# Stick-breaking weights as products of sigmoids, and two projections by blocks, in a two-block fp32 network

## Chip, cores and metric

The kernel runs on one core of one Trainium2 chip. The metric is the device time in microseconds of one execution, the median of several. PE is TensorE, DVE is VectorE, ACT is ScalarE, POOL is GpSimd, SP is the queue that issues the DMAs.

## What is computed

256 tokens of width 1024 pass through two transformer-like blocks, all in fp32. The first block multiplies a normalised input with a projection of some 15,000 columns and feeds three branches: an mLSTM with four heads of 256, a short convolution, and stick-breaking attention with 16 heads of 64. The change touches the first and the last of these:

```python
# stick-breaking attention, per head; mask[t, s] = s < t
z = einsum('bhqd,bshd->bhqs', qblk, kf)            # q scaled by d ** -0.5
log_beta = log_sigmoid(z)
log_1m = where(mask, log_beta - z, 0.0)
cum = cumsum(log_1m, axis=-1)
log_a = log_beta + cum[..., -1:] - cum
a = where(mask, exp(log_a), 0.0)                   # = sigmoid(z_ts) * prod_{s<j<t} (1 - sigmoid(z_tj))
out = einsum('bhqs,bshd->bqhd', a, vf)

# mLSTM
y_ml = head_rmsnorm(sigmoid(ml_o) * h_tilde, ml_norm_g, ML_HEADS)
```

Gated projections of the branches, an MLP with squared ReLU, and a second block (recurrent, gated-linear and block-sparse attention branches and a gated MLP) follow and are not touched.

## The kernel before

**Groups and units.** `plan_groups` cuts all products with weights into groups of 512 output columns; a group is worked off in units of up to four blocks of 128 rows of the contraction. A weight tile of a unit (128x2048) is loaded by SP into one of three landing buffers, copied by ACT to a rounded leading part `whi` (L1132), and DVE subtracts to get the rest `wlo` (L1566, `split`); both parts have a ring of three. The activations are split the same way, and PE adds three products: leading by leading, leading by rest, rest by leading. A "tok" group (L594 to L596) has tokens on the output's partitions and moves 512 columns per matmul, 24 matmuls a unit. A "feat" group (L602 to L606) has features there and moves 256 columns, 48 matmuls a unit. A third form, `chunk_product`, is used for the groups `sbk`, `mlq` and `mlk`: for each chunk of 128 features, four matmuls of 512 columns multiply `whi` with both parts of the activations side by side (L561), and four of 256 columns `wlo` with the leading part (L566); DVE then adds the two halves with a reduce for each chunk (`take_chunk`, L1625) before it scales the group (L2038).

**Order.** Every engine walks through the units `u = 0, 1, 2, ...`; what else it does is written out between them by the number of the unit. PE runs the product of unit u and then the extra work of u; `between(u, k)` puts work inside a product, before its k-th block. ACT and DVE start an iteration with a few steps, then prepare the weights of unit u+2, then do the rest of the iteration. The split of unit u+2 can begin once PE has finished unit u-1. The units 0 to 11 are `sbq`, `sbk`, `sbv`; `SB0` is 12. Units 12 to 19 are `mlq0`, `mlq1`, `mlk0`, `mlk1`, 20 to 27 `mlv0`, `mlv1`, `mlo0`, `mlo1` (token form), 28 to 31 `scc0`, `scc1` (feature form); `ML0`, where the mLSTM heads begin, is 30.

**Stick-breaking, two heads at a time, with i = u - SB0.** PSUM has four spare banks `M[0..3]`; head h lives in `M[h % 4]`.
- PE, even i: `sb_scores(i)` (L780, L783): the scores with keys on partitions, 384 columns a head, in three 128x128 blocks (the fourth is above the diagonal).
- ACT, odd i: `sb_logs` (L1208 to L1211): Abs, Exp, then Ln, each over 384 elements, with a table load between.
- DVE: `sb_softplus` (L1637); POOL: `keep` (L2278) zeroes the masked half of the two diagonal blocks by an affine select over 256 elements.
- ACT, next even i: `sb_leading` rounds to `sbw_hi` (L1217), DVE: `sb_rest` subtracts (L1642), and PE, at the end of that unit: `sb_remain` (L793, L794) adds the cumulated sums onto the scores by matmuls with a triangle of minus ones and a block of minus ones, for both parts.
- ACT, odd i: `sb_weights` (L1223) takes Exp; POOL masks again; PE, at the end of the odd unit: `sb_values` (L802, L805). Then ACT and DVE take the result in two parts (`sb_result`, L1227, L1647).

PE's order at the end of an even unit is so remainder (heads i-2, i-1), scores (heads i, i+1), and at the end of an odd one values.

**mLSTM output gate.** ACT computes Exp of the negated, scaled `mlo` (L1442); in the units 28 to 31 DVE adds one and takes the reciprocal over 512 elements (`output_gate`, L1677, L1678).

Of the kernel before, what the change touches and what calls it, by code (L numbers as in the profile page):

```python
# [5 lines left out]
F32 = mybir.dt.float32  # L6
# [151 lines left out]
def chunked(name):  # L158

    return name[:3] in ("sbk", "mlq", "mlk")  # L160
# [31 lines left out]
GATE0 = SB0 + SB_H  # L192
# [6 lines left out]
def build(nc, dram, out):  # L199
# [25 lines left out]
    minus_rstd = sb("minus_rstd", [P, TT], side="right")  # L225
# [38 lines left out]
    sbw_hi = sb("sbw_hi", [P, 2, 3 * P], F32R, stack=area)  # L264
    sbw_lo = sb("sbw_lo", [P, 2, 3 * P], F32R, stack=area)
    sums_r = sb("sums_r", [P, 2 * P], F32R, stack=area)
# [17 lines left out]
    sbw = sb("sbw", [P, 2, 3 * P], stack=mix)  # L284
# [66 lines left out]
    def banks(name):  # L351
# [22 lines left out]
    half_in, ones_in, heat_set, minus_ready = (sem(n) for n in ("half_in", "ones_in", "heat_set", "minus_ready"))  # L374
# [7 lines left out]
    sums_ready, sb_hi, sb_lo = sem("sums_ready"), sem("sb_hi"), sem("sb_lo")  # L382
    sb_z, sb_log, sb_t, sb_tm, sb_r, sb_a, sb_am, sb_av, sb_y = (
        sem(n) for n in ("sb_z", "sb_log", "sb_t", "sb_tm", "sb_r", "sb_a", "sb_am", "sb_av", "sb_y"))
# [109 lines left out]
    def _(pe):  # L494
# [271 lines left out]
        def sb_scores(h):  # L766
# [11 lines left out]
            for i in range(2):  # L778
                hs = slice(SB_D * i, SB_D * (i + 1))
                mm(M[(h + i) % 4][:, 0:T], sbkT[hs, c, 0:P], sbqT[hs, c, :], start=True, stop=True)  # L780
            for i in range(2):
                hs = slice(SB_D * i, SB_D * (i + 1))
                mm(M[(h + i) % 4][:, T:T + P], sbkT[hs, c, P:T], sbqT[hs, c, P:T], start=False, stop=True,  # L783
                   skip_group_check=True).then_inc(sb_z, 1)
# [12 lines left out]
        def sb_values(h):  # L797

            pe.wait_ge(sb_am, h + 2)
            to = M[h % 4]  # L800
            for i in range(2):
                mm(to[SB_D * i:SB_D * (i + 1), 0:T], sbv[:, 0, (h + i) * SB_D:(h + i + 1) * SB_D],  # L802
                   sba[:, i, 0:T], start=True, stop=False, skip_group_check=True)
            for i in range(2):
                last = mm(to[SB_D * i:SB_D * (i + 1), P:T], sbv[:, 1, (h + i) * SB_D:(h + i + 1) * SB_D],  # L805
                          sba[:, i, T:3 * P], start=False, stop=True, skip_group_check=True)
# [19 lines left out]
        def ml_scores(h):  # L826
            s, b = M[2 * (h % 2)], M[2 * (h % 2) + 1]
            if h < 2:
                pe.wait_ge(sb_a, SB_H)
# [158 lines left out]
        def between(u, k):  # L988


            if (u, k) == (LAST_U["psc1"], 2):
# [65 lines left out]
        for u in range(NU):  # L1057
# [54 lines left out]
    def _(act):  # L1112
# [89 lines left out]
        def sb_logs(h):  # L1202

            for i in (h, h + 1):
                act.wait_ge(sb_z, i + 1)
                if i >= 2:
                    act.wait_ge(sb_lo, i - 1)
                link(activate(sbw[:, i % 2], M[i % 4][:, 0:3 * P], ACT.Abs))  # L1208
                link(activate(sbw[:, i % 2], sbw[:, i % 2], ACT.Exp, scale=-1.0))
            for i in (h, h + 1):  # L1210
                activate(sbw[:, i % 2], sbw[:, i % 2], ACT.Ln, bias=1.0).then_inc(sb_log, 1)  # L1211

        def sb_leading(h):
            act.wait_ge(sb_tm, h + 1)
            if h >= 2:
                act.wait_ge(sb_r, h - 1)
            activate(sbw_hi[:, h % 2], sbw[:, h % 2], ACT.Copy).then_inc(sb_hi, 1)  # L1217

# [1181 lines left out]
```

## Time and profile before

| | |
|---|---|
| median of 3 runs | 915.6 us (915.51 to 915.62) |
| the profiled execution | 915.87 us, its span 914.2 us |
| PE busy | 903.5 us, 99% of the span |
| DVE / ACT / POOL busy | 605.8 / 489.0 / 44.3 us |
| HBM read | 162 MB, 181 GB/s over the span |
| remainder, scores and values of the 16 heads | between 87 and 208 us of the span |

The span is what the profiler sees of the program; the execution's time holds a little more on either side. Matmuls are pipelined: the duration in a row is the time from a matmul's start to its modelled end, and several are under way at once.

### The profile page before, as it was taken

How to read it: one execution, taken by the hardware profiler on the slowest of the kernel's cores; microseconds unless marked ns; L12 is line 12 of the kernel's file. 1: busy time of each engine (PE TensorE's matmuls, PEld its weight loads, DVE VectorE, ACT ScalarE, POOL GpSimd, SP SyncE). 2: the span in 40 equal slices, each digit the busy share in tenths (PEclk: the TensorE clock that was granted, in tenths of full speed). 3: DMA queues.
4: the chain of work that ended last, by engine and by line, in shares of the span. 5: the costliest groups of instructions: out<-in, count | busy, mean ns of one | idle time of the engine just before them, and what ended most of it. 6: DMA issues, size and time to landing. Idle time of an engine off the chain costs nothing. (4 is left out here: it accounts for less than half of the span.)

```text
span 914.2 us, 12499 instructions
## 1 busy us (share of the span) xinstructions
PE 903.5 (99%) x5137; PEld 779.1 (85%) x5137; DVE 605.8 (66%) x637; ACT 489.0 (53%) x570; POOL 44.3 (5%) x79
## 2 busy tenths in 40 slices
PE   8999999999999999999999999999999999999997
PEld 7988887789998888888888888889987888888886
DVE  5776766567887445556677755557796677777643
ACT  6434787873435433345555543537777765555441
POOL 1110111110010000000000000001000010000000
PEclk9999999999999999999999999999999999999999
DMA  9676453444255565555565556544842475556641
GB/s 301 221 247 214 138 177 125 160 138 139 92 184 184 186 203 201 194 190 201 167 199 187 185 194 203 201 141 144 277 139 92 132 237 185 184 185 207 207 162 47
DMA packets 99438, 163.92 MB, mean 179 GB/s; under 512 B 4856, under 2 KB 37384, under 8 KB 99253
## 3 DMA queue, kind: packets, MB, share of 16 engines
q1 hardware_dynamic: 99380, 163.11, 54.5%
q8 instruction: 41, 0.67, 0.3%
q14 instruction: 17, 0.13, 0.0%
HBM read 162.04 MB, written 3.16 MB: 181 GB/s over the span
## 5 line engine op out<-in xcount | busy, mean ns | idle before, releaser
L1566 DVE TENSOR_TENSOR wlo<-land,whi 128x2048 fp32r<-128x2048 f32 (+2 forms) x152 | 334.9, 2206 | 164.2 <-ACT whi L1132 163.8
L1132 ACT ACTIVATE whi<-land 128x2048 fp32r<-128x2048 f32 (+1 forms) x152 | 280.3, 1847 | 202.1 <-PE acc L596 145.6
L602 PE MATMUL acc<-xT,whi 128*128 128x256 f32 x336 | 97.2, 289 | 0.0
L606 PE MATMUL acc<-xT,wlo 128*128 128x256 f32 x336 | 95.1, 283 | 0.0
L604 PE MATMUL acc<-xT,whi 128*128 128x256 f32 x336 | 95.0, 283 | 0.0
L594 PE MATMUL acc<-whi,xT 128*128 128x512 f32 (+2 forms) x240 | 91.6, 382 | 0.0
L595 PE MATMUL acc<-wlo,xT 128*128 128x512 f32 (+2 forms) x240 | 90.3, 376 | 0.0
L596 PE MATMUL acc<-whi,xT 128*128 128x512 f32 (+2 forms) x240 | 90.1, 376 | 0.0
L637 PE MATMUL acc<-xT,whi 128*128 128x512 f32 x288 | 69.4, 391 | 0.2 <-DVE gu L2234 0.2
L637 PE MATMUL m<-xT,whi 128*128 128x512 f32 x288 | 68.7, 391 | 0.0
L602 PEld LDWEIGHTS acc<-xT,whi 128*128 128x128 f32 x336 | 64.3, 191 | 2.9 <-issue 2.6
L604 PEld LDWEIGHTS acc<-xT,whi 128*128 128x128 f32 x336 | 64.4, 192 | 0.2
L606 PEld LDWEIGHTS acc<-xT,wlo 128*128 128x128 f32 x336 | 64.4, 192 | 0.0
L637 PEld LDWEIGHTS acc<-xT,whi 128*128 128x128 f32 x288 | 52.8, 188 | 10.5 <-DVE gu L2234 0.4
L637 PEld LDWEIGHTS m<-xT,whi 128*128 128x128 f32 x288 | 52.9, 188 | 10.2
L594 PEld LDWEIGHTS acc<-whi,xT 128*128 128x128 f32 x240 | 45.1, 188 | 9.6 <-issue 1.0
L561 PE MATMUL acc<-xT,whi 128*128 128x512 f32 x192 | 53.0, 397 | 0.0
L596 PEld LDWEIGHTS acc<-whi,xT 128*128 128x128 f32 x240 | 45.1, 188 | 8.2
L595 PEld LDWEIGHTS acc<-wlo,xT 128*128 128x128 f32 x240 | 45.1, 188 | 7.7
L594 PE MATMUL acc<-whi,aT_hi 128*128 128x512 f32 x128 | 49.9, 390 | 0.0
L595 PE MATMUL acc<-wlo,aT_hi 128*128 128x512 f32 x128 | 49.8, 389 | 0.0
L596 PE MATMUL acc<-whi,aT_lo 128*128 128x512 f32 x128 | 49.8, 389 | 0.0
(410 smaller groups left out, 1515.0 us busy)
## 6 DMA issues: line engine op xcount, KB each, us to landing
land<-in_w_in SPq DMA_DIRECT2D x55, 1024.0 KB, 5.2
land<-in_w_up SPq DMA_DIRECT2D x16, 1024.0 KB, 5.2
land<-in_w_down SPq DMA_DIRECT2D x16, 1024.0 KB, 5.1
land<-in_w_ffn_gate SPq DMA_DIRECT2D x22, 512.0 KB, 4.1
land<-in_w_ffn_up SPq DMA_DIRECT2D x22, 512.0 KB, 5.3
land<-in_w_ffn_down SPq DMA_DIRECT2D x10, 1024.0 KB, 5.0
land<-in_w_in SPq DMA_DIRECT2D x14, 512.0 KB, 4.7
land<-in_w_out SPq DMA_DIRECT2D x6, 1024.0 KB, 5.0
```

Of the source, the lines that this page charges most:

```text
L561: mm(to, whi[:, s, k, cs], xT[:, k0 + k].rearrange("p a t -> p (a t)"), start=k0 + k == 0, stop=False, skip_group_check=True)
L594: mm(to, xh[:, k0 + k, ts], whi[:, s, k, 0:w], start=first, stop=False)
L595: mm(to, xh[:, k0 + k, ts], wlo[:, s, k, 0:w], start=False, stop=False)
L596: last = mm(to, xl[:, k0 + k, ts], whi[:, s, k, 0:w], start=False, stop=end)
L602: mm(to, whi[:, s, k, cs], xh[:, k0 + k, :], start=first and c % 2 == 0, stop=False, skip_group_check=True)
L604: mm(to, whi[:, s, k, cs], xl[:, k0 + k, :], start=False, stop=False, skip_group_check=True)
L606: last = mm(to, wlo[:, s, k, cs], xh[:, k0 + k, :], start=False, stop=end, skip_group_check=True)
L637: mm(to[:, c, :], whi[:, s, k, c * P:(c + 1) * P], xT[:, k0 + k].rearrange("p a t -> p (a t)"), start=k0 + k == 0, stop=False, skip_group_ ...
L1132: activate(whi[:, u % PARTS, 0:m, 0:w], land[:, u % LANDS, 0:m, 0:w], ACT.Copy).then_inc(hi_ready, 1)
L1566: v.tensor_tensor(wlo[:, u % PARTS, 0:m, 0:w], land[:, u % LANDS, 0:m, 0:w], whi[:, u % PARTS, 0:m, 0:w].bitcast(F32), ALU.subtract).then_ ...
```

## The change

- The scores are computed with queries on the partitions (operands of `sb_scores` swapped), the same number of matmuls and columns.
- `sb_logs`, `sb_leading`, `sb_weights`, `sb_softplus`, `sb_rest`, `sb_remain` and the buffers `sbw_hi`, `sbw_lo`, `sums_r` go.
- ACT: `sb_sigmoids` writes `sigmoid(-z)` to `sbw` and `sigmoid(z)` to `sba`, 384 elements each, two heads, at the start of an odd iteration.
- POOL: `keep` sets the masked part of `sbw` to 1 and that of `sba` to 0, two selects a head.
- DVE: `sb_products`: a scan from the last key to the first multiplies the factors (`renew` restarts the product at the border between the two query blocks), then a product with `sba`. It stands at the start of an odd iteration, ahead of the weight split.
- PE: `sb_turn`, six transposes (three a head) after the first block of the next even unit's product; ACT copies the results out of PSUM (`sb_copy`); `sb_values` stands at the end of that even unit, directly ahead of the scores of the next pair. So a pair is through one unit sooner.
- `mlq` and `mlk` become plain feature-form groups; DVE scales them from PSUM, without the reduces.
- The output gate is ACT's Sigmoid, and DVE's addition and reciprocal go.

```diff
 def chunked(name):
-    return name[:3] in ("sbk", "mlq", "mlk")
+    return name[:3] == "sbk"
...
@@ tensor
-        def sb_remain(h):
-
-            if h == 0:
-                pe.wait_ge(sums_ready, 1)
-            pe.wait_ge(sb_lo, h + 1)
-            z = M[h % 4]
-            for w in (sbw_hi[:, h % 2], sbw_lo[:, h % 2]):
-                mm(z[:, 0:3 * P], sums_r[:, 0:P], w, start=False, stop=True, skip_group_check=True)
-                last = mm(z[:, P:T], sums_r[:, P:], w[:, T:3 * P], start=False, stop=True, skip_group_check=True)
-            last.then_inc(sb_r, 1)
+        def sb_turn(h):
+
+            pe.wait_ge(sb_a, h + 1)
+            for i in range(3):
+                last = nc.tensor.transpose(M[h % 4][:, i * P:(i + 1) * P], sba[:, h % 2, i * P:(i + 1) * P], ident)
+            last.then_inc(sb_at, 1)
...
         def between(u, k):
+            if k == 1 and u - SB0 in range(2, SB_H + 1, 2):
+                sb_turn(u - SB0 - 2)
+                sb_turn(u - SB0 - 1)
...
-            if i % 2 == 0 and 0 <= i <= SB_H:
-                if i >= 2:
-                    sb_remain(i - 2)
-                    sb_remain(i - 1)
-                if i < SB_H:
-                    sb_scores(i)
-            if i % 2 == 1 and 3 <= i <= SB_H + 1:
-                sb_values(i - 3)
+            if i % 2 == 0 and 2 <= i <= SB_H:
+                sb_values(i - 2)
+            if i % 2 == 0 and 0 <= i < SB_H:
+                sb_scores(i)
@@ scalar
+        def sb_sigmoids(h):
 
             for i in (h, h + 1):
                 act.wait_ge(sb_z, i + 1)
                 if i >= 2:
-                    act.wait_ge(sb_lo, i - 1)
-                link(activate(sbw[:, i % 2], M[i % 4][:, 0:3 * P], ACT.Abs))
-                link(activate(sbw[:, i % 2], sbw[:, i % 2], ACT.Exp, scale=-1.0))
+                    act.wait_ge(sb_a, i - 1)
+                    act.wait_ge(sb_at, i - 1)
+                activate(sbw[:, i % 2], M[i % 4][:, 0:3 * P], ACT.Sigmoid, scale=-1.0)
+                activate(sba[:, i % 2], M[i % 4][:, 0:3 * P], ACT.Sigmoid).then_inc(sb_sig, 1)
+
+        def sb_copy(h):
             for i in (h, h + 1):
+                act.wait_ge(sb_at, i + 1)
+                if i >= 2:
+                    act.wait_ge(sb_av, i // 2)
+                activate(sbaT[:, i % 2], M[i % 4][:, 0:3 * P], ACT.Copy).then_inc(sb_ac, 1)
@@ vector
+        def sb_products(h):
+
+            if h == 0:
+                dve.wait_ge(sb_set, 2)
+            dve.wait_ge(sb_kept, 2 * h + 1)
+            link(v.tensor_tensor_scan(sbp[:, h % 2, ::-1], sbw1[:, h % 2, 3 * P:0:-1], renew[:, ::-1], 1.0, ALU.mult,
+                                      ALU.max))
+            dve.wait_ge(sb_kept, 2 * h + 2)
+            v.tensor_tensor(sba[:, h % 2], sba[:, h % 2], sbp[:, h % 2], ALU.mult).then_inc(sb_a, 1)
...
+            if u - SB0 in range(1, SB_H, 2):
+                sb_products(u - SB0 - 1)
+                sb_products(u - SB0)
@@ gpsimd
+        for h in range(SB_H):
+            pool.wait_ge(sb_sig, h + 1)
+            signal(keep(sbw[:, h % 2], ALU.is_gt, -1, 1.0), sb_kept)
+            signal(keep(sba[:, h % 2], ALU.is_gt, -1), sb_kept)
```

How PE's queue moves, at the end of unit 14 and of unit 15. Before:

```order
L566 MATMUL acc<-xT,wlo 128x256 x4
L793 MATMUL m<-sbw_hi,sums_r 128x384
L794 MATMUL m<-sbw_hi,sums_r 128x128
L793 MATMUL m<-sbw_lo,sums_r 128x384
L794 MATMUL m<-sbw_lo,sums_r 128x128
...
L780 MATMUL m<-sbqT,sbkT 128x256 x2
L783 MATMUL m<-sbqT,sbkT 128x128 x2
L561 MATMUL acc<-xT,whi 128x512 x4
...
L802 MATMUL m<-sba,sbv 64x256 x2
L805 MATMUL m<-sba,sbv 64x128 x2
```

The four remainder rows stand twice, once a head. PE's queue now, in unit 14 after its first block of rows, and at the end of the same unit:

```order
L604 MATMUL acc<-xT,wlo 128x256
L788 MATMUL m<-lead,sba 128x128 x6
L600 MATMUL acc<-xT,whi 128x256
L602 MATMUL acc<-xT,whi 128x256
...
L796 MATMUL m<-sbaT,sbv 64x256 x2
L799 MATMUL m<-sbaT,sbv 64x128 x2
L778 MATMUL m<-sbkT,sbqT 128x256 x2
L781 MATMUL m<-sbkT,sbqT 128x128 x2
```

The remainder has left the end of the even unit, the transposes have come into its middle, and the values have moved up from the odd unit to stand ahead of the scores.

DVE's queue for one pair of units (14 and 15) before, with its waits; `land`, `whi`, `wlo` belong to the weights:

```order
L1566 TENSOR_TENSOR wlo<-land,whi 128x2048 [waits landed1,hi_ready]
L1642 TENSOR_TENSOR sbw_lo<-sbw,sbw_hi 128x384 [waits sb_hi] x2
L1566 TENSOR_TENSOR wlo<-land,whi 128x2048 [waits landed2,hi_ready]
L1625 TENSOR_REDUCE mlqT<-acc 128x256 [waits chunk_done] x2
L1637 SCALAR_TENSOR_TENSOR sbw<-m,sbw 128x384 [waits sb_log] x2
L1625 TENSOR_REDUCE mlqT<-acc 128x256 [waits chunk_done]
L1625 TENSOR_REDUCE mlqT<-acc 128x256 [waits units_done]
L2038 SCALAR_TENSOR_TENSOR mlqT<-mlqT,row 128x1024 [waits chunk_read]
```

and now (the scan is the row that writes `sbp`):

```order
L1546 TENSOR_TENSOR wlo<-land,whi 128x2048 [waits landed1,hi_ready]
L1625 TENSOR_TENSOR ysbT_lo<-m,ysbT_hi 128x256 [waits sb_y_hi]
L1618 SCALAR_TENSOR_TENSOR sbp<-sbw,renew 128x384 [waits sb_kept]
L1621 TENSOR_TENSOR sba<-sba,sbp 128x384 [waits sb_kept,dve_step]
L1618 SCALAR_TENSOR_TENSOR sbp<-sbw,renew 128x384 [waits sb_kept]
L1621 TENSOR_TENSOR sba<-sba,sbp 128x384 [waits sb_kept,dve_step]
L1546 TENSOR_TENSOR wlo<-land,whi 128x2048 [waits landed2,hi_ready]
L2014 SCALAR_TENSOR_TENSOR mlqT<-acc,row 128x1024 [waits units_done]
```

The `sbw` work and the reduces are gone; scans and products wait for POOL's `sb_kept` ahead of the weight split of unit 17.

## Rows read from the trace of the kernel before

**Rows 1.** the page: busy time, share and instructions of each engine; the granted clock

```profile
PE 903.5 (99%) x5137; PEld 779.1 (85%) x5137; DVE 605.8 (66%) x637; ACT 489.0 (53%) x570; POOL 44.3 (5%) x79
...
PEclk9999999999999999999999999999999999999999
```

**Rows 2.** waits of PE and its weight loads: us in total, times, longest

```profile
PE m L793 <- DVE sbw_lo L1642: 0.2, 1, 0.2
...
PEld m L793 <- DVE sbw_lo L1642: 1.0, 2, 0.7
```

**Rows 3.** PE timeline after unit 14: start, us, then the instruction

```profile
99.52 0.41 PE L793 MATMUL m<-sbw_hi,sums_r 128*128 128x384 f32 x1
...
100.78 0.70 PE L780 MATMUL m<-sbqT,sbkT 64*128 64x256 f32 x4
...
101.64 1.20 PE L561 MATMUL acc<-xT,whi 128*128 128x512 f32 x4
```

**Rows 4.** PE timeline after unit 22, token form

```profile
157.69 0.33 PE L793 MATMUL m<-sbw_hi,sums_r 128*128 128x384 f32 x1
...
158.87 0.70 PE L780 MATMUL m<-sbqT,sbkT 64*128 64x256 f32 x4
```

**Rows 5.** PE timeline after unit 20: the hole before the remainder

```profile
142.84 0.39 PE L596 MATMUL acc<-whi,xT 128*128 128x512 f32 x1
143.47 0.45 PE L793 MATMUL m<-sbw_hi,sums_r 128*128 128x384 f32 x1 [0.24 <-DVE sbw_lo L1642]
```

**Rows 6.** PE timeline in the second block: six transposes in either stream

```profile
685.99 0.82 PE L876 MATMUL m<-lead,mbs 128*128 128x128 f32 x6
...
686.76 0.28 PE L604 MATMUL acc<-xT,whi 128*128 128x256 f32 x1
...
708.38 0.82 PE L876 MATMUL m<-lead,mbs 128*128 128x128 f32 x6
...
709.27 0.40 PE L595 MATMUL acc<-wlo,y2T_hi 128*128 128x512 f32 x1
```

**Rows 7.** PE timeline after unit 15: a values block

```profile
107.44 0.65 PE L802 MATMUL m<-sba,sbv 128*64 128x256 f32 x4
...
108.24 0.96 PE L561 MATMUL acc<-xT,whi 128*128 128x512 f32 x3
```

**Rows 8.** PE timeline: a chunked unit from its start to the next, and plain matmuls

```profile
36.53 1.09 PE L561 MATMUL acc<-xT,whi 128*128 128x512 f32 x4
...
42.15 1.09 PE L561 MATMUL acc<-xT,whi 128*128 128x512 f32 x4
...
198.83 0.28 PE L602 MATMUL acc<-xT,whi 128*128 128x256 f32 x1
...
200.15 0.28 PE L606 MATMUL acc<-xT,wlo 128*128 128x256 f32 x1
```

**Rows 9.** single lines' instructions: count, ns min/median/max, first and last start

```profile
L1208 ACT ACTIVATE sbw<-m x16: 470/492/500, 89.2 to 189.8; 128x384 f32<-128x384 f32 x16
...
L1211 ACT ACT_TABLE_LOAD  x8: 1283/1283/1283, 91.4 to 190.9; - x8
...
L2278 POOL TENSOR_SCALAR_AFFINE_SELECT sba<-sba x20: 406/408/2083, 103.5 to 241.9; 128x256 f32<-128x256 f32 x20
...
L1642 DVE TENSOR_TENSOR sbw_lo<-sbw,sbw_hi x16: 548/550/553, 98.8 to 199.4; 128x384 fp32r<-128x384 f32 x16
...
L1837 DVE TENSOR_TENSOR_SCAN lw<-lw x2: 664/678/691, 685.9 to 686.5; 128x256 f32<-128x256 f32 x2
```

**Rows 10.** PE timeline in unit 20: 512-column matmuls, eighteen steps

```profile
138.30 0.39 PE L594 MATMUL acc<-whi,xT 128*128 128x512 f32 x1
...
142.39 0.39 PE L594 MATMUL acc<-whi,xT 128*128 128x512 f32 x1
```

**Rows 11.** GpSimd's and VectorE's timelines at 188 us

```profile
188.59 2.56 POOL L2278 TENSOR_SCALAR_AFFINE_SELECT sba<-sba 128x256 f32<-128x256 f32 x2 [6.97 <-ACT sba L1223]
...
188.12 2.29 DVE L1566 TENSOR_TENSOR wlo<-land,whi 128x2048 fp32r<-128x2048 f32 x1 [2.25 <-ACT whi L1132]
```

More of the change, by code:

```diff
@@ L263, in build @@
     early.close()
-    sbw_hi = sb("sbw_hi", [P, 2, 3 * P], F32R, stack=area)
-    sbw_lo = sb("sbw_lo", [P, 2, 3 * P], F32R, stack=area)
-    sums_r = sb("sums_r", [P, 2 * P], F32R, stack=area)
+    sbaT = sb("sbaT", [P, 2, 3 * P], stack=area)
+    sbp = sb("sbp", [P, 2, 3 * P], stack=area)
+    renew = sb("renew", [P, 3 * P], stack=area)
     area.close()
@@ L283, in build @@
     mlo = sb("mlo", [P, TT, D], stack=mix)
-    sbw = sb("sbw", [P, 2, 3 * P], stack=mix)
+    sbw1 = sb("sbw", [P, 2, 3 * P + 1], stack=mix)
+    sbw = sbw1[:, :, 0:3 * P]
     sba = sb("sba", [P, 2, 3 * P], stack=mix)
@@ L1376, in _ @@
                 square(5, x_tok, tok[:, 0, 0:NG], (1,))
-            if u - SB0 in range(4, SB_H + 3, 2):
-                sb_result(u - SB0 - 4)
+            if u - SB0 in range(3, SB_H + 2, 2):
+                sb_result(u - SB0 - 3)
+            if u - SB0 in range(1, SB_H, 2):
+                sb_sigmoids(u - SB0 - 1)
             if u == B2 + 4:
@@ L1439, in _ @@
                 product_done(f"mlo{j}")
-                act.wait_ge(minus_ready, 1)
+                act.wait_ge(rstd_ready, 1)
                 for t in range(TT):
-                    last = activate(mlo[:, t, j * NG:(j + 1) * NG], acc[:, SIDE[G_AT[f"mlo{j}"]], t], ACT.Exp,
-                                    scale=minus_rstd[:, t:t + 1])
+                    last = activate(mlo[:, t, j * NG:(j + 1) * NG], acc[:, SIDE[G_AT[f"mlo{j}"]], t], ACT.Sigmoid,
+                                    scale=rstd[:, 0, t:t + 1])
                 last.then_inc(read_act, 1)
-            if i % 2 == 1 and 3 <= i <= SB_H + 1:
-                sb_weights(i - 3)
-                sb_weights(i - 2)
-            if i % 2 == 1 and 1 <= i < SB_H:
-                sb_logs(i - 1)
             i = u - ML0
@@ L1623, in take_chunk @@
             k = 4 * j + c
-            to = {"sbk": sbkT, "mlq": mlqT, "mlk": mlkT}[name[:3]][:, k, :]
-            v.tensor_reduce(to, acc[:, (SIDE[n] + c // 2) % 2, c % 2, :].rearrange("p (a t) -> p t a", a=2), AX.X,
+            v.tensor_reduce(sbkT[:, k, :], acc[:, (SIDE[n] + c // 2) % 2, c % 2, :].rearrange("p (a t) -> p t a", a=2), AX.X,
                             ALU.add).then_inc(chunk_read, 1)
@@ L1943, in _ @@
                 make_diag(2, 5)
[L1944 to L1945 removed]
+            if u - SB0 in range(3, SB_H + 2, 2):
+                sb_result(u - SB0 - 3)
+            if u - SB0 in range(1, SB_H, 2):
+                sb_products(u - SB0 - 1)
+                sb_products(u - SB0)
             if u == B2 + 2:
@@ L2273, in inverse_root, with keep @@
                                    ALU.pow), rstd_ready)
-        def keep(view, above):
+        def keep(view, above, free=1, fill=0.0):
             w = view.rearrange("p (a c) -> p a c", c=P)[:, 0:3:2, :]
-            return g.affine_select(out=w, in_=w, pattern=[[0, 2], [1, P]], compare_op=above, fill=0.0, base=0,
-                                   channel_multiplier=-1)
+            return g.affine_select(out=w, in_=w, pattern=[[0, 2], [free, P]], compare_op=above, fill=fill, base=0,
+                                   channel_multiplier=-free)
         signal(g.memset(ymlT_hi[:, 0:2, :].bitcast(F32), 1.0), heat_set)
@@ L2294, in _ @@
                                m_parts[0:ML_H, :].bitcast(F32), ALU.subtract), m_split)
-        for i in range(0, SB_H + 2, 2):
-            if i >= 2:
-                for h in (i - 2, i - 1):
-                    pool.wait_ge(sb_a, h + 1)
-                    signal(keep(sba[:, h % 2], ALU.is_gt), sb_am)
-            if i < SB_H:
-                for h in (i, i + 1):
-                    pool.wait_ge(sb_t, h + 1)
-                    signal(keep(sbw[:, h % 2], ALU.is_gt), sb_tm)
+        for h in range(SB_H):
+            pool.wait_ge(sb_sig, h + 1)
+            signal(keep(sbw[:, h % 2], ALU.is_gt, -1, 1.0), sb_kept)
+            signal(keep(sba[:, h % 2], ALU.is_gt, -1), sb_kept)
         for h in range(ML_H):
```

70 lines of the change are left out of this document (17 added, 53 removed).

## The prediction

> **What bounds the kernel.** I read the page first: PE is busy 99% of the span at the full granted clock, which is the 2.4 GHz level, from the first slice to the last [rows 1]. Then the waits of PE: in the whole program the only wait that belongs to the code of this change is the one of the first remainder matmul for `sbw_lo`, three times, 1.2 us in all with the weight loads counted [rows 2]. The kernel is therefore a queue of matmuls without holes, and an edit is worth what it takes out of that queue or puts in, plus any new hole. Last I read PE's timeline. The duration printed for a matmul is its latency, 0.28 to 0.40 us; its price in a full queue is the distance between starts, and all prices below are such distances.
>
> **The change part by part.** The work in question lies in units 12 to 29, from about 87 to 208 us.
>
> 1. The remainder matmuls go: eight instructions per pair of heads, eight pairs. Between chunked units the block takes from 99.52 to 100.78, 1.26 us [rows 3]; between token-form units from 157.69 to 158.87, 1.18 us [rows 4]. Four blocks stand near each kind; the eight measure 9.8 us. Term: -9.8.
>
> 2. The hole in front of them goes. Before the block at 143.47 the last matmul began at 142.84 and the next could have begun 0.23 later, so 0.40 us was lost, of which the view counts 0.24 as idle [rows 5]; a second hole of about 0.2 stands before another pair. The waits view allows 1.2 [rows 2]. I take -0.6, the part seen as a gap between starts, and keep 0 and -1.2 as ends.
>
> 3. Six transposes per pair come in, in the middle of an even unit. The same instruction, six 128x128 transposes of fp32 against the identity, stands in the second block. In a stream of 256-column matmuls it displaces 685.99 to 686.76, less one regular step of 0.12: 0.65 us. In a stream of 512-column matmuls 708.38 to 709.27, less 0.23: 0.66 us [rows 6]. Eight of them: +5.3, with 4.6 (the bare 0.57 a block without its effect on the next matmul) and 6.4 (0.80, if these cost as much as a values block) as ends.
>
> 4. The values and the scores come to stand side by side. The values alone cost 107.44 to 108.24 and leave the next matmul late [rows 7]; a change of operand shape costs about 0.1 at each edge. Seven pairs of blocks lose one pair of edges, but get a seam of their own, as there is one between remainder and scores. Term: -0.7; ends 0 and -1.3.
>
> 5. mlq and mlk, eight units, are multiplied in the plain form. A chunked unit goes from 36.53 to 42.15, 5.62 us. Plain matmuls of 256 columns follow each other at 0.120 (198.83 to 200.15, eleven steps), and 48 make 5.76 [rows 8]. Term: +1.1; ends 0.8 and 1.3.
>
> 6. VectorE loses 16 reduces, 32 `sbw` steps and four reciprocals with their additions; ScalarE loses Abs, Exp and Ln of every head and nearly all table loads of the stretch [rows 9]. PE waits for none of them but `sbw_lo`, already counted, so these are worth nothing: the matmul queue covers them, and would have to shrink by microseconds per unit before they showed. The weight split is queued behind the new VectorE products, since `sb_products` stands ahead of `split` in an odd unit. It then ends about 8.6 us after the scores (6.3 from step 7, and 2.3 for the split itself), while PE wants it after two units and the blocks between them, 14 us. Nothing.
>
> 7. The new chain is the one place for a new hole. From the scores (T0) it runs: ScalarE two sigmoids a head, GpSimd two masks a head, VectorE a scan and a product a head, then the transposes. Prices: 0.49 for a pass of 384 elements out of PSUM, 0.41 for a mask, 0.55 for a product of two SBUF operands [rows 9]. No scan of 384 elements is in the trace; scans of 256 take 0.68 [rows 9]. In proportion that is 1.02, and a scan cannot well be under the 0.55 of a plain pass; the upper end is open until measured, and I keep 2.0. With engines overlapping the second head is ready at 0.98 (two sigmoids) + 0.41 + 2 x (1.02 + 0.55) = 4.5 us, about 5 with ten hand-overs of 0.05. If GpSimd and VectorE never overlap: 0.98 + 4 x 0.41 + 2 x 1.57 = 5.8, 6.3 with the hand-overs. PE comes to the transposes after one unit and a quarter: 60 steps of 0.120, 7.2 us, in the first three pairs and the last; 30 steps of 0.227 (138.30 to 142.39, eighteen steps) [rows 10], 6.8 us, in the others. So no hole is left, with 0.5 us to spare at worst and 2 at best. The Sigmoid table has to be loaded once, 1.28 us [rows 9], for the first pair; ScalarE is idle before those scores, so I count nothing and keep 0.4 as the upper end. After the transposes ScalarE's two copies (about 1 us) have three quarters of a unit, 4.1 us. The copies wait behind a weight split, which is over before the transposes are.
>
> That GpSimd and VectorE shut each other out is visible: of twenty masks with a median of 0.41 us one took 2.08 [rows 9]. It belongs to the pair at 188.59, which fell under VectorE's subtraction of two SBUF operands, begun at 188.12 and 2.29 long, and ended after that did [rows 11]. The Trainium skill says the same of operations with two SBUF inputs (SBUF — State Buffer, section Who interferes with whom): one side holds the pair for the whole instruction, the other waits. By this rule scans, products and masks all line up, which is the 6.3 us above and not the 5; the trace agrees.
>
> Sum: -9.8 - 0.6 + 5.3 - 0.7 + 1.1 = **-4.7 us**. The profiled execution took 915.87 us, its span 914.2. So 911.2 as this execution would be; the median of the three runs is 0.3 lower, and I say **910.9 us**.
>
> **The rivals.** The measurement can tell about 0.2%, 1.8 us, from no change.
>
> (a) The chain is late and PE waits at the transposes: slower. It decides at one place, the wait for `sb_a` in unit 14 and each second unit after it. If the scan of 384 elements, read backwards and with a second operand, takes 2.0 instead of 1.02, the fully lined-up chain is 0.98 + 1.64 + 2 x 2.55 + 0.5 = 8.2 us, 1.0 late in four pairs and 1.4 late in four: 9.6 us, and the time is 920.5. It turns the sign from a mean lateness of 4.7 / 8 = 0.6 us, so from scans of about 1.7. For it: no scan of this length or direction is in the trace, and both sides share GpSimd's masks. Against it: three places with scans of 256 all show 0.68. The Trainium skill (DVE: opcode table, instruction layouts, handler registers and perf-mode slots, section Datapath and trigger behaviour) says that a scan runs at half throughput; by that the 384 elements would take about 1 us, and the trace agrees. Chance 0.05.
>
> (b) Small lateness eats the gain: ten hand-overs of 0.15 instead of 0.05 and a scan of 1.2 make the lined-up chain 0.98 + 1.64 + 2 x 1.75 + 1.5 = 7.6, late by 0.4 and 0.8, 4.8 us in all, and less where the engines do overlap. All of it gives 915.7, no change; half of it 913.3. Chance 0.10.
>
> (c) The transposes and seams are cheaper than I priced them: every lower end together, -9.8 - 1.2 + 4.6 - 1.3 + 0.8 = -6.9, 908.7 us. Nothing speaks for all ends at once; a part of it is likely. Chance 0.12.
>
> (d) The projections by blocks cost more than their steps, because the plain form waits for both halves of the weights before its first matmul. Before, the halves were ready long before PE wanted them: the view in which [rows 2] stand has no wait of PE for `whi` or `wlo` in that stretch. Chance 0.02, price 1 to 2 us.
>
> **How the numbers follow.** Forecast 0.71, at 910.9; rivals 0.05, 0.10, 0.12, 0.02. Its own bounds, not all at one end, give 909.6 to 912.4. The range reaches half way into (c) and to the gentle half of (b): 909.2 to 913.2; outside are (a), half of (b) and the far part of (c), about 0.17. Faster by over 0.2% (below 913.8) has the forecast, (c), half of (b) and (d): 0.90. Within 0.2%: the other half of (b), 0.05. Slower: (a), 0.05.
>
> **What would show it.** Right: PE's waits name nothing in units 12 to 29; six transposes displace about 0.65 us; from one scores block to the next there are about 14.0 us in the plain units (14.5 to 14.7 before, chunked) and 13.5 in the token-form ones (14.1 before). GpSimd's masks are drawn out by scans. The spans before unit 12 and after unit 30 have the same length as before. Wrong: a wait of PE for `sba`, a scan over 1.5 us, or a gain found outside units 12 to 29.

## The result

The changed kernel takes 910.55 us (910.15 to 910.99, five runs), the kernel before 915.6 us beside it; the ratio is 0.9947, with a 95% interval of 0.9936 to 0.9958. The prediction was 910.9, with a range of 909.2 to 913.2.

The page of the changed kernel, against [rows 1]: the busy times and the granted clock.

```profile
PE 898.4 (99%) x5249; PEld 781.2 (86%) x5249; DVE 590.2 (65%) x616; ACT 453.5 (50%) x523; POOL 53.3 (6%) x78
...
PEclk9999999999999999999999999999999999999999
```

PE is still busy for 99%, at the full granted clock. The view of waits, by PE alone (us in total, times, longest), against [rows 2]:

```profile
PE acc L961 <- POOL ymlT_hi L2255: 1.4, 1, 1.4
PE acc L651 <- DVE whi L1884: 1.4, 1, 1.4
PE m L698 <- DVE x_tok L1877: 0.6, 1, 0.6
PE acc L718 <- ACT xT L1161: 0.4, 1, 0.4
PE m L760 <- DVE diag L1565: 0.3, 1, 0.3
PE acc L635 <- DVE gu L2208: 0.2, 1, 0.2
```

None of these is in the stretch of the change (between 86 and 209 us the view by PE is empty): the wait for `sbw_lo` is gone and none for `sba` or `sbaT` has come. PE's timeline of unit 14 and the first steps of unit 15 (start, us, instruction), against [rows 3], [rows 6] and [rows 7]:

```profile
94.85 0.82 PE L788 MATMUL m<-lead,sba 128*128 128x128 f32 x6
95.42 0.36 PE L600 MATMUL acc<-xT,whi 128*128 128x256 f32 x1
95.62 0.28 PE L602 MATMUL acc<-xT,whi 128*128 128x256 f32 x1
...
99.69 0.28 PE L604 MATMUL acc<-xT,wlo 128*128 128x256 f32 x1
99.90 0.65 PE L796 MATMUL m<-sbaT,sbv 128*64 128x256 f32 x4
...
100.70 0.70 PE L778 MATMUL m<-sbkT,sbqT 64*128 64x256 f32 x4
...
101.55 0.39 PE L600 MATMUL acc<-xT,whi 128*128 128x256 f32 x1
101.78 0.28 PE L602 MATMUL acc<-xT,whi 128*128 128x256 f32 x1
```

Six transposes displace 94.85 to 95.62 less one step of 0.12, 0.65 us, as the same instruction did in the second block. From its own start to the start of what follows a block of values takes 0.80 us and a block of scores 0.85. Around the two stand delays that belong to neither: 0.09 ahead (99.69 to 99.90 for a step of 0.12) and about 0.1 behind (101.55 to 101.78, again for 0.12). Ahead of the transposes there is none: they begin one regular step after the matmul before them.

**A measure that is finer than the whole time.** The first scores start at 87.26 in the profiled execution of the kernel before and at 86.70 in that of the changed one; in all the executions below they lie between 86.4 and 87.7, whatever was changed after them. This scatter of the start is not the change's. What follows the region took between 700.21 and 700.26 us in all fourteen profiled executions. I therefore measure from the start of the first scores to the start of the first mLSTM scores (L836 before, L829 after) and call it the region. It covers units 13 to 30 and the blocks between them. Each row below is a kernel of the section on experiments:

| kernel | region, us | median, us | median of before beside it, us |
|---|---|---|---|
| before | 126.65 | | 915.6 |
| changed | 121.50 | 910.55 | 915.6 |
| blocks alone | 126.43 | 915.51 | 915.32 |
| gate alone | 126.64 | 915.50 | 915.41 |
| short remainder | 122.78 | 911.78 | 915.41 |
| no remainder | 116.74 | 905.63 | 915.33 |
| short transposes | 118.19 | 907.38 | 915.41 |
| values apart | 122.99 | 911.83 | 915.38 |
| scan twice | 122.28 | 911.49 | 915.41 |
| scan three times | 134.85 | 923.75 | 915.33 |
| table early | 121.50 | 910.92 | 915.33 |
| chunks, naive order | 140.93 | 928.52 | 915.32 |
| chunks, reduces early | 121.14 | 910.30 | 915.32 |
| chunks, reduces and table early | 120.44 | 908.95 | 915.33 |

The region gained 5.15 us. That is the whole gain of the medians, 5.05, within their scatter. Behind the region the two kernels are equal (700.24 and 700.23), so nothing was gained or lost there.

The chain of one pair (heads 2 and 3) on POOL and on DVE, where PE's scores begin at 100.70 and end, by the row of L781, at 101.62:

```profile
102.73 0.41 POOL L2252 TENSOR_SCALAR_AFFINE_SELECT sbw<-sbw 128x256 f32<-128x256 f32 x1 [10.08 <-ACT sba L1202]
103.20 1.12 POOL L2252 TENSOR_SCALAR_AFFINE_SELECT sba<-sba 128x256 f32<-128x256 f32 x1
104.47 0.79 POOL L2252 TENSOR_SCALAR_AFFINE_SELECT sbw<-sbw 128x256 f32<-128x256 f32 x1
105.33 1.12 POOL L2252 TENSOR_SCALAR_AFFINE_SELECT sba<-sba 128x256 f32<-128x256 f32 x1
```

```profile
103.17 0.96 DVE L1618 TENSOR_TENSOR_SCAN sbp<-sbw,renew 128x384 f32<-128x384 f32 x1 [1.51 <-POOL sbw L2252]
104.43 0.56 DVE L1621 TENSOR_TENSOR sba<-sba,sbp 128x384 f32<-128x384 f32 x1 [0.31 <-POOL sba L2252]
105.29 0.96 DVE L1618 TENSOR_TENSOR_SCAN sbp<-sbw,renew 128x384 f32<-128x384 f32 x1 [0.30 <-POOL sbw L2252]
106.55 0.56 DVE L1621 TENSOR_TENSOR sba<-sba,sbp 128x384 f32<-128x384 f32 x1 [0.30 <-POOL sba L2252]
```

The scan of 384 elements takes 0.96 us. A mask of 0.41 that starts 0.03 after a scan ends 0.19 after it, so it takes 1.12, and DVE idles 0.3 for it. The two engines do not work side by side there, and the last product ends at 107.11, 5.5 us after the scores. PE begins the transposes at 108.84, 1.7 us later. In the token-form pairs, where PE gets there sooner (scores end at 143.35, products at 148.84, transposes at 150.25), it is 1.4. The true margin is 0.33 larger, 2.1 and 1.7 us, because the first three transposes need only the first head's product, and the fourth, which needs the last one, starts 0.33 after the first.

In the first pair the order of starts was the other way round, and there the scan was held up:

```profile
90.55 0.41 POOL L2252 TENSOR_SCALAR_AFFINE_SELECT sba<-sba 128x256 f32<-128x256 f32 x1
```

```profile
90.59 1.18 DVE L1618 TENSOR_TENSOR_SCAN sbp<-sbw,renew 128x384 f32<-128x384 f32 x1 [4.68 <-POOL sbw L2252]
```

This mask began just before the scan and kept its 0.41, and the scan took 1.18 in place of 0.96.

### The profile page after: what moved, and what is told of

Same layout as the page of the kernel before. It is cut to its first block and busy times, and to the rows that moved or that the text cites. A ratio compares the mean times of both kernels' runs of the same rounds, so it can differ in the third digit from the quotient of the medians.

```text
span 908.4 us, 12654 instructions
## 1 busy us (share of the span) xinstructions
PE 898.4 (99%) x5249; PEld 781.2 (86%) x5249; DVE 590.2 (65%) x616; ACT 453.5 (50%) x523; POOL 53.3 (6%) x78
## 5 line engine op out<-in xcount | busy, mean ns | idle before, releaser
L600 PE MATMUL acc<-xT,whi 128*128 128x256 f32 x464 | 134.1, 289 | 0.0
L602 PE MATMUL acc<-xT,whi 128*128 128x256 f32 x464 | 131.4, 283 | 0.0
L604 PE MATMUL acc<-xT,wlo 128*128 128x256 f32 x464 | 131.3, 283 | 0.0
L600 PEld LDWEIGHTS acc<-xT,whi 128*128 128x128 f32 x464 | 88.9, 192 | 3.3 <-issue 2.4
L602 PEld LDWEIGHTS acc<-xT,whi 128*128 128x128 f32 x464 | 89.0, 192 | 0.3
L604 PEld LDWEIGHTS acc<-xT,wlo 128*128 128x128 f32 x464 | 88.9, 192 | 0.0
L635 PE MATMUL acc<-xT,whi 128*128 128x512 f32 x288 | 69.4, 392 | 0.2 <-DVE gu L2208 0.2
L635 PEld LDWEIGHTS acc<-xT,whi 128*128 128x128 f32 x288 | 52.8, 188 | 10.5 <-DVE gu L2208 0.4
L640 PEld LDWEIGHTS acc<-xT,wlo 128*128 128x128 f32 x288 | 37.2, 191 | 1.6
```

The lines of the kernel that those rows point to most:

```text
L600: mm(to, whi[:, s, k, cs], xh[:, k0 + k, :], start=first and c % 2 == 0, stop=False, skip_group_check=True)
L602: mm(to, whi[:, s, k, cs], xl[:, k0 + k, :], start=False, stop=False, skip_group_check=True)
L604: last = mm(to, wlo[:, s, k, cs], xh[:, k0 + k, :], start=False, stop=end, skip_group_check=True)
L635: mm(to[:, c, :], whi[:, s, k, c * P:(c + 1) * P], xT[:, k0 + k].rearrange("p a t -> p (a t)"), start=k0 + k == 0, stop=False, skip_group_ ...
L640: last = mm(to[:, c, 0:T], wlo[:, s, k, c * P:(c + 1) * P], xT_hi[:, k0 + k, :], start=False, stop=k0 + k == kk - 1, skip_group_check=True)
```

## Experiments

**One part alone: the form of the projections.** The kernel before with

```diff
-    return name[:3] in ("sbk", "mlq", "mlk")
+    return name[:3] == "sbk"
```

> The kernel before with mlq and mlk in the plain form, nothing else. Term 5 of the prediction alone: plus 1.1 us by the steps. Term 2 (the hole before the remainder comes from a VectorE that is late with its subtraction): without sixteen reduces the holes after units 16 and 18 close, minus 0.2. Together 916.5; first scores to first mLSTM scores 127.5 us instead of 126.65. Rival: the plain form waits for both weight halves and costs more, 918; or VectorE's relief is worth more than the steps, under 915.6.

Measured: 915.51 beside 915.32 (ratio 1.0001, 0.9992 to 1.001), region 126.43, 0.2 less than before. The expected rise did not come. In the view of PE's timeline no hole is marked any more, and the pair that held the one of 0.40 us shrank from 14.72 to 14.35; next to plain matmuls the remainder block also has no delay in front, where it had 0.08 behind a chunk (99.52 in [rows 3] is 0.20 after the last matmul before it, for a step of 0.12):

```profile
100.06 0.28 PE L606 MATMUL acc<-xT,wlo 128*128 128x256 f32 x1
100.18 0.34 PE L793 MATMUL m<-sbw_hi,sums_r 128*128 128x384 f32 x1
```

So on top of the kernel before, the plain form costs about what it frees. What it costs by itself is seen further down.

**One part alone: the output gate.**

```diff
-                    last = activate(mlo[...], acc[...], ACT.Exp, scale=minus_rstd[:, t:t + 1])
+                    last = activate(mlo[...], acc[...], ACT.Sigmoid, scale=rstd[:, 0, t:t + 1])
...
-            link(v.tensor_scalar(o, o, 1.0, None, ALU.add))
-            link(v.reciprocal(o, o))
```

> The kernel before with the output gate as ScalarE's Sigmoid and without VectorE's addition and reciprocal (15.1 us of VectorE's time), nothing else. Theory (VectorE is off the path): no change, 915.6 within 0.5; PE's timeline keeps its steps. Rival (VectorE's relief in units 28 to 31 lets PE go on sooner): 914 or less.

Measured: 915.50 beside 915.41, region 126.64 against 126.65. 15 us of VectorE's time (605.8 us busy before, 590.9 here) were worth nothing.

**The remainder block shortened, then taken away with its chain.**

```diff
-            for w in (sbw_hi[:, h % 2], sbw_lo[:, h % 2]):
-                mm(z[:, 0:3 * P], sums_r[:, 0:P], w, start=False, stop=True, skip_group_check=True)
+            for w in (sbw_lo[:, h % 2],):
                 last = mm(z[:, P:T], sums_r[:, P:], w[:, T:3 * P], start=False, stop=True, skip_group_check=True)
```

> The kernel before with one matmul of 128 columns a head in place of the four remainder matmuls; it leaves out most of the cumulated sums. Term 1 by itself: a block of 1.18 to 1.30 us becomes about 0.3, so 8 times 0.95, about 7.6 us under 915.6: 908.0. Rival (the block is partly hidden and PE waits elsewhere instead): less than 5 us.

Measured: 911.78 beside 915.41, region 122.78. Only 3.9 us of the expected 7.6 came, and the rival was right about where the rest is. PE's timeline there:

```profile
113.35 0.80 PE L793 MATMUL m<-sbw_lo,sums_r 128*128 128x128 f32 x2 [0.73 <-DVE sbw_lo L1641]
...
142.01 0.79 PE L793 MATMUL m<-sbw_lo,sums_r 128*128 128x128 f32 x2 [0.87 <-DVE sbw_lo L1641]
...
155.67 0.33 PE L793 MATMUL m<-sbw_lo,sums_r 128*128 128x128 f32 x2
```

The view of waits has the first remainder row of this kernel behind DVE's subtraction (us, times, longest), for the weight loads and the matmuls:

```profile
PEld m L793 <- DVE sbw_lo L1641: 4.3, 8, 1.3
...
PE m L793 <- DVE sbw_lo L1641: 1.9, 3, 0.9
```

6.2 us in place of the 1.2 of [rows 2], though part of this is the same time seen twice, by the weight load and by its matmul. By the distances between starts PE lost 4.4 us at these rows. About 2.0 of it stands ahead of the second head's matmul, 0.3 to 0.4 us in five pairs: there the matmuls that went had covered DVE's second subtraction. The other 2.4 stands ahead of the first head's (0.9, 1.0 and 0.5 in three pairs): PE now reaches the block before DVE, whose subtraction stands behind a weight split of 2.28 us. The second experiment takes the rounding and the subtraction away too, and the masks release the weights directly:

```diff
-                    sb_remain(i - 2)
-                    sb_remain(i - 1)
...
-                    act.wait_ge(sb_lo, i - 1)
+                    act.wait_ge(sb_tm, i - 1)
...
-            act.wait_ge(sb_r, h + 1)
+            act.wait_ge(sb_tm, h + 1)
...
-                sb_leading(i - 2)
-                sb_leading(i - 1)
...
-                sb_rest(i - 2)
-                sb_rest(i - 1)
```

> The kernel before without the remainder matmuls and without the rounding and subtraction that feed them; it leaves out the cumulated sums. One matmul a head in their place saved only 3.8 us, and PE waited for sbw_lo in most pairs. Theory: the block was in part cover for VectorE's late second half, so without that chain terms 1 and 2 come out whole: 9.8 + 0.6, region 126.65 to about 116.2 us, time 905.0. Rival (the block is worth no more than what the short one gave): about 911.

Measured: 905.63 beside 915.33, region 116.74: 9.9 us, where terms 1 and 2 say 10.4. The missing 0.5 is in the token-form pairs: there the distance from scores to scores fell from 14.11 to 13.05, so by 1.06 and not by the 1.18 of [rows 4]. Before, the remainder followed the 512-column matmuls without a delay (0.23, one step); now the scores stand there and start 0.32 after the last one. So the block is worth what its starts say, but only to a change that also removes what PE would wait for.

**The transposes shortened**, `for i in range(3)` to `for i in range(1)` in `sb_turn`.

> The changed kernel with one transpose a head in place of three; the other two thirds of the weights are not transposed. Term 3 by itself: 32 transposes at 0.57 / 6 = 0.095 us: 3.0 us under 910.55, 907.5. Rival (the price of a transposes block is its edges): no more than 1 us.

Measured: 907.38, region 118.19, 3.3 us less than that of the changed kernel: 32 transposes at 0.103 us. All 48 are then 5.0, and the delay of the matmul behind them makes up the rest of eight times 0.65, 5.2.

**The values apart from the scores**, the seam by itself.

```diff
-            if i % 2 == 0 and 2 <= i <= SB_H:
-                sb_values(i - 2)
+            if i % 2 == 1 and 3 <= i <= SB_H + 1:
+                sb_values(i - 3)
...
-            if u - SB0 in range(3, SB_H + 2, 2):
-                sb_result(u - SB0 - 3)
+            if u - SB0 in range(4, SB_H + 3, 2):
+                sb_result(u - SB0 - 4)
```

> The changed kernel with the values at the end of the odd unit, as before, apart from the scores; results one unit later. Term 4 by itself. By the prediction the seam is worth 0.1 us a pair, 0.7 in all: first scores to first mLSTM scores 122.2 us against 121.5. Rival: the kernel before without its remainder block took 116.74, and 5.0 to 5.3 for the transposes and 1.06 for the plain form on top leave 1.3 to 1.5 for the merging, 0.2 a pair: 122.9. Neither is beyond the scatter of the whole time; the region decides.

Measured: 911.83, region 122.99; the rival. PE's timeline at the end of unit 15 of this kernel:

```profile
106.64 0.28 PE L604 MATMUL acc<-xT,wlo 128*128 128x256 f32 x1
106.85 0.65 PE L796 MATMUL m<-sbaT,sbv 128*64 128x256 f32 x4
...
107.65 0.39 PE L600 MATMUL acc<-xT,whi 128*128 128x256 f32 x1
107.87 0.28 PE L602 MATMUL acc<-xT,whi 128*128 128x256 f32 x1
```

A block of values or of scores between two matmuls of 0.12 costs 0.09 ahead of it (106.85 for 106.76) and 0.10 behind it (0.22 for 0.12). Side by side the two blocks pay this once, and the seam between values and scores costs nothing beyond the 0.80 that a values block takes in any place. From scores to scores that saves 0.18 to 0.19 us in the plain stretches (14.17 against 13.99) and 0.26 in the token-form ones (13.73 against 13.47), where the matmuls behind a block stay a little further apart for a few steps. Four and three of them make the 1.5 of the region. The delays belong to these blocks and not to every interruption: the remainder (in plain or token-form matmuls) and the transposes, whose operands fill 128*128 in the rows, had none ahead of them, while the scores have 64*128 and the values 128*64.

**The margin of the new chain.** The scan done twice, then three times (`for _ in range(2)` and `range(3)` around it).

> The changed kernel with every scan done twice. It tests the margin of step 7: the chain from the scores ends at 5.5 us and gets 1.9 longer, 7.4, PE reaches the transposes at 7.2 in four pairs and 6.8 in four. Theory: PE waits for sba about 0.3 and 0.7 us, 4 us in all: 914.5. Rival (the chain is nowhere near the path): 910.5; rival (hand-overs and the lock make the chain longer than I count): over 918.

> The changed kernel with every scan done three times. With two scans the chain of a pair with the table in place ended 6.8 us after the scores, 0.4 before PE, and only the first pair waited. A third scan adds 1.92: 8.7 us. Theory (the margin is used up, from here each scan costs its full time): first pair 1.9 more, three pairs with plain matmuls 1.5 each, four in token form 1.9 each, 14 us over the kernel with two scans: 925; PE waits for sba in all eight pairs. Rival (slack elsewhere takes up the wait): under 918.

Two scans: 911.49, region 122.28, only 0.8 more. DVE's, POOL's and PE's rows for the second pair, and PE's for the first:

```profile
104.65 1.97 DVE L1619 TENSOR_TENSOR_SCAN sbp<-sbw,renew 128x384 f32<-128x384 f32 x2 [1.52 <-POOL sbw L2253]
106.65 0.58 DVE L1622 TENSOR_TENSOR sba<-sba,sbp 128x384 f32<-128x384 f32 x1
107.15 2.15 DVE L1619 TENSOR_TENSOR_SCAN sbp<-sbw,renew 128x384 f32<-128x384 f32 x2
109.33 0.56 DVE L1622 TENSOR_TENSOR sba<-sba,sbp 128x384 f32<-128x384 f32 x1
```

```profile
104.69 1.12 POOL L2253 TENSOR_SCALAR_AFFINE_SELECT sba<-sba 128x256 f32<-128x256 f32 x1
```

```profile
96.60 0.55 PE L788 MATMUL m<-lead,sba 128*128 128x128 f32 x3 [0.56 <-DVE sba L1622]
...
110.32 0.82 PE L788 MATMUL m<-lead,sba 128*128 128x128 f32 x6
```

The last product ends at 109.89, 6.8 us after the scores, and PE comes to the transposes at 110.32. The chain grew by 1.3, not by the 1.9 of the two added scans: the mask that the first scan held up ends beside the second scan (at 105.81), so DVE's three idle times of 0.3 are gone, while the second head's scans, begun under a mask, took 2.15. Only the first pair waits, because ACT loads the Sigmoid table after the wait for the scores. Three scans: 923.75, region 134.85, so 12.6 us over two scans, where 14 was expected. PE's row for the second pair, and below it the rows of the view of waits (us, times, longest):

```profile
114.60 0.55 PE L788 MATMUL m<-lead,sba 128*128 128x128 f32 x3 [0.92 <-DVE sba L1622]
```

```profile
PEld m L788 <- DVE sba L1622: 12.2, 8, 2.8
PE m L788 <- DVE sba L1622: 10.3, 8, 2.5
```

All eight pairs wait now, and the waits stand ahead of the fourth transpose, the first of the second head. The expectation reckoned with the first transpose, which is 0.33 us earlier. With two scans the last product was ready 0.4 to 0.8 us before that fourth transpose was due; the third scan made the chain 1.8 longer (8.6 us), and behind the first pair PE lost 1.1 us in each of three pairs and 1.3 to 1.4 in each of four. So beyond the margin a microsecond of the chain costs a microsecond of the time in each pair. By the distances between starts the holes are 10.8 us of the 12.6. About 1.3 more went to the clock: behind the first pair's hole of 2.7 us the granted clock was at the lower level of 1.2 GHz from 97.65 to 101.06, and behind the seven later holes of 1.1 to 1.4 us it stayed at 2.4 GHz.

**The table alone**, a tiny Sigmoid on ACT ahead of the first scores.

```diff
             if i == 0:
                 act.wait_ge(tab_out, 16)
+                activate(root[:, 0:1], ident[:, 0:1], ACT.Sigmoid)
```

> The changed kernel with the tiny Sigmoid alone. The first pair's chain gets 1.28 us shorter, but it ended 0.8 us before PE anyway: no change, 910.5, region 121.5. Rival (the first pair was on the path): 1 us less.

Measured: 910.92, region 121.50, the same to the last digit.

**The chunked form with the new weights.** The changed kernel with

```diff
-    return name[:3] == "sbk"
+    return name[:3] in ("sbk", "mlq", "mlk")
...
             for c in range(NG // P):
                 to, cs = acc[:, (SIDE[n] + c // 2) % 2, c % 2, :], slice(c * P, (c + 1) * P)
+                if c == 1:
+                    between(u, 1)
```

and the chunk's target chosen by name again.

> The changed kernel with mlq and mlk chunked again; the transposes of units 14, 16 and 18 stand after the first chunk; VectorE's order is otherwise that of the change, so all four reduces of a group stand behind the stick-breaking products and the weight split. Theory 1 (chunks save 0.14 us a unit, but the products hold VectorE): the products end 5.5 us after the scores, the split 2.3 later, so the first reduce is done at 8.5 us, while PE wants the chunk's bank at 5.7. PE waits about 2.7 us at units 14, 16 and 18 and about 3.4 at unit 20, less 1.1 for the steps: about 920. Theory 2 (form of the product is free of VectorE, only the steps count): 909.4. A wait of PE for mlqT and mlkT tells them apart.

Measured: 928.52 beside 915.32 (ratio 1.0131, 1.0112 to 1.0149), region 140.93. PE's timeline has its four holes, and the view by stretches (us, busy time by engine, then PE's granted clock, DMA share and GB/s) the clock:

```profile
97.10 1.16 PE L561 MATMUL acc<-xT,whi 128*128 128x512 f32 x4 [3.52 <-issue]
...
115.24 1.70 PE L561 MATMUL acc<-xT,whi 128*128 128x512 f32 x4 [2.60 <-issue]
...
133.39 2.04 PE L561 MATMUL acc<-xT,whi 128*128 128x512 f32 x4 [2.62 <-issue]
...
153.33 0.80 PE L594 MATMUL acc<-whi,xT 128*128 128x512 f32 x1 [3.17 <-DVE mlkT L1606]
```

```profile
87.00:108.00 21.00, 17.48 (x100) 14.72 (x101) 11.84 (x12) 9.12 (x13) 2.35 (x5) 0.92 0.45 149
108.00:120.00 12.00, 9.40 (x47) 8.18 (x46) 10.66 (x11) 5.20 (x6) 3.39 (x4) 0.86 0.27 87
120.00:140.00 20.00, 17.38 (x93) 14.71 (x92) 11.87 (x13) 6.72 (x9) 3.45 (x4) 0.83 0.35 107
```

The holes stand where theory 1 has them, 11.9 us as the rows count them. The profile names DVE's reduce as what ended the wait only for the last; for the other three it names nothing, but the matmul at 97.10 starts 0.1 us after DVE's first reduce of `mlqT` has ended (96.32 to 97.00), and the next experiment moves the reduces and removes the holes. The region is 19.4 us longer than the changed kernel's. The other 7.5 us, and the 1 us that the chunks save, went to the clock, which no expectation had: in these stretches the mean granted clock is 0.92, 0.86 and 0.83, so PE was part of the time at the lower level of 1.2 GHz. That level holds for 3.4 to 6.8 us at each hole, 17 us in all, the last time until 156.60; at half speed that loses some 8 us. From there to the end of the region it is 1.00. The executions differ in this: the mean granted clock of the whole program was 0.989 in the slowest of the four (929.71, the profiled one) and 0.995 in the fastest (924.79). The Trainium skill (TensorE: Matmul & The Clock Gate, Why this matters for your kernels) warns that gaps between bursts of matmuls bring the clock down; the trace agrees, for holes of 2.6 to 3.5 us that come every 18 us.

Then the reduces are moved:

```diff
+            early = ends and chunked(name) and u > SB0
+            if early:
+                take_chunk(name, 0)
             if u - SB0 in range(1, SB_H, 2):
                 sb_products(u - SB0 - 1)
+                if early:
+                    take_chunk(name, 1)
                 sb_products(u - SB0)
...
-            if ends and chunked(name):
+            if ends and chunked(name) and not early:
```

> As before this one, but VectorE takes the first chunk ahead of the products and the second between the two heads' products. Theory 1: the reduces come in time, the chain ends about 6.4 us after the scores instead of 5.5, before PE reaches the transposes at 7.1; what is left is the price of the steps, 8 units by 0.14: 1.1 us under the changed kernel, about 909.4. Rival: the later chain or a late second half of the reduces makes PE wait, 911 or more.

Measured: 910.3, region 121.14. One hole is left, in the first pair; PE's row, and DVE's before it:

```profile
98.01 1.19 PE L561 MATMUL acc<-xT,whi 128*128 128x512 f32 x4 [0.42 <-DVE mlqT L1606]
```

```profile
95.07 2.29 DVE L1548 TENSOR_TENSOR wlo<-land,whi 128x2048 fp32r<-128x2048 f32 x1
97.27 1.28 DVE L1606 TENSOR_REDUCE mlqT<-acc 128x256 f32<-128x512 f32 x2
```

The third chunk's reduce stands behind the products and the split, and those are late by the table load. With that loaded early:

> The changed kernel with chunked mlq and mlk, the reduces put ahead of and between the products, and one tiny Sigmoid on ScalarE ahead of the first scores, so that the table is loaded before them. In the run without it the first pair's chain held the second half of the reduces and PE lost 0.7 us at unit 14. Theory: that loss goes, first scores to first mLSTM scores 120.4 us against 121.5 of the changed kernel; time 909.4. Rival: PE waits at the same place for another reason, 121.1.

Measured: 908.95 (908.88 to 909.17, five runs), region 120.44, beside 915.33 (ratio 0.9929, 0.9915 to 0.9942). Beside the same runs of the kernel before, the changed kernel with the table alone took 910.92 (910.67 to 911.4), so these ranges do not touch. This version beats both kernels, and the difference of the regions, 1.06 us, is the price of the plain form in eight units.

## Why the prediction was right

**The bound.** PE's queue without holes set the time before and sets it now. What did not touch the queue was worth nothing: the gate (region 126.64 for 126.65) and the table.

The number came out 0.4 us from the forecast, and that closeness is in part luck: terms 1 and 2 were 0.5 too large together and term 4 was 0.8 too small, and the two misses point in opposite directions.

**Terms 1 and 2** (-9.8 and -0.6): together -9.9 by the kernel without the remainder; in the token-form pairs the scores inherit a delay ahead of them that the remainder did not have. The reason for leaving the terms at full value was thinner than I wrote. I counted 1.2 us of waits as all that DVE owed; the short remainder shows that the block itself kept PE from outrunning DVE, and that three quarters of its matmuls removed without the chain give only 3.9 us. The change removes the chain too, which is why the sum held.

**Term 3** (+5.3): six transposes displace 0.65 us, as predicted from the second block, so eight blocks 5.2. What the other measured terms leave of the region, -5.15 + 9.9 + 1.5 - 1.06, is 5.2 as well, so nothing is left unexplained.

**Term 4** (-0.7): mis-sized, it is -1.5. I let the merged blocks "get a seam of their own"; there is none, and in the token-form stretches an interruption costs 0.26 and not 0.2. Rival (c), which had -1.3 as this term's end, was right about it.

**Term 5** (+1.1): +1.06, from the chunked version of the changed kernel. In the kernel before it was paid back by shorter holes and edges.

So the sum is -9.9 + 5.2 - 1.5 + 1.1 = -5.1, for a forecast of -4.7. That the delays go with the shape of the operands is read from the rows; no kernel here changed a block's shape and nothing else.

**Step 6** held: DVE's split of unit 17 ends at 109.3 in the changed kernel, 7.7 us after the scores (8.6 forecast), and PE never waits for it. From one scores block to the next it is 14.00 us in the plain units (86.70 to 100.70) and 13.48 in the token-form ones (142.42 to 155.90), for a forecast of 14.0 and 13.5.

**Step 7** held. The last product comes 1.4 to 1.7 us before the first transpose, inside my 0.5 to 2, and the scan took 0.96 for my 1.02. The chain of 5.5 us lies between my two forms, 5 and 6.3: I added whole masks to whole scans, while of a held mask DVE sees only an idle time of 0.3. Rival (a) was priced too high for the same reason, and because the last product is needed 0.33 later than I reckoned. It had the sign turn at scans of 1.7 us and 920.5 for scans of 2.0; with 1.97 us of scans a head the kernel took 911.49. Only three scans, 2.9 us, made the chain late in every pair, at 923.75. One reason given was wrong: the first pair's table load is not hidden in ACT's idle time. In ACT's timeline it comes after the wait for the scores:

```profile
87.70 1.28 ACT L1201 ACT_TABLE_LOAD   x1 [4.67 <-PE m L781]
89.00 0.49 ACT L1201 ACTIVATE sbw<-m 128x384 f32<-128x384 f32 x1
```

It cost nothing only because the first pair had the time to spare: even with the load its last product ends at 94.05, 0.8 us before the transposes at 94.85. Rival (b) asked for hand-overs of 0.15 throughout. They lie between 0.03 (GpSimd to VectorE) and 0.20 us (ScalarE to GpSimd), and the chain has room for them. Rival (d): no wait of PE for `whi` or `wlo` stands in the region, and the plain form alone left its length as it was.

The rule of the Trainium skill on operations with two SBUF inputs (SBUF — State Buffer, Who interferes with whom) described the masks and scans of one pair: it says that they contend, and that the order of issue decides who is blocked. The trace agrees with both, by the mask of 1.12 us behind the start of a scan and the scan of 1.18 behind the start of a mask. That the other side waits for the whole instruction, which my prediction took over, it says of VectorE's two-port modes. The kernel with two scans shows less than that here: the mask that the first scan had held up ended at 105.81, in the middle of the second, and the two scans took 1.97 us for twice 0.96, so the end of that mask did not hold up the second scan.

## What to carry to other kernels

In a queue without holes price an edit by the distances between starts, and read the delays ahead of a block and behind it too: a block of scores or values cost 0.19 us here besides its contents in 256-column matmuls and 0.26 in 512-column ones, and two such blocks put side by side pay it once. What stands next to the place of a removed block can inherit its delays. Before removing work from the bounding engine, ask which late partner it covers, and remove that partner's chain with it. Where a new chain is put in front of other work on a shared engine, let what the bounding engine wants first go first: the same chunked products were 1.3% slower than the kernel before with the reduces behind the chain, 0.5% faster with them ahead, and 0.7% faster with the table loaded early as well.

## What the runs showed of the hardware

- Holes of 2.6 to 3.5 us, four in 60 us, cost the matmul clock: mean granted clock 0.83 to 0.92 in those stretches, some 8 us on top of 12 us of holes. One hole of 2.7 us (three scans, first pair) cost it too, about 1.3 us; seven holes of 1.1 to 1.4 us in the same kernel did not.
- A scores or values block (operands 64*128 and 128*64) in a stream of 256-column matmuls starts 0.09 us late and leaves the next matmul 0.10 late. Six transposes (128*128) start on time and displace 0.65 us.
- A scan of 384 fp32 elements, read backwards, takes 0.96 us on VectorE, and 1.15 to 1.18 when a GpSimd mask was begun before it; 256 take 0.68.
- A GpSimd mask of 0.41 us under a scan ended 0.19 us after the scan, both when VectorE then idled and when a second scan followed at once.
- The start of the first scores scatters by 1.3 us between executions of kernels whose matmuls are the same up to there. The region after it repeats to 0.01 us where nothing on PE's path was changed (121.50 twice, 126.65 and 126.64), and the rest of the span to 0.05.
